# Prompt's merge products behind the sample's tiles, one block from merge to experts, and an output stage with the gate product first

## What is computed

```python
def encoder_layer(x, c, w_ada, b_ada, ...):
    mod = jax.nn.silu(c) @ w_ada + b_ada
    sh1, sc1, ga1, sh2, sc2, ga2 = jnp.split(mod[:, None, :], 6, axis=-1)
    h = rms_norm(x, g_pre1) * (1.0 + sc1) + sh1
    u = h @ w_in
    ...
    y_ret = retention_mixer(qr, kr, vr, gr, gn_ret)
    y_hg = hgrn2_mixer(qh, ih, ffh, fbh, gh, lb, gn_hg)
    merged = jax.nn.sigmoid(za) * (y_ret @ w_br_ret) + jax.nn.sigmoid(zb) * (y_hg @ w_br_hg)
    x = x + ga1 * rms_norm(merged @ w_out, g_post1)
    h2 = rms_norm(x, g_pre2) * (1.0 + sc2) + sh2
    x = x + ga2 * rms_norm(expert_choice_ffn(h2, w_router, w_gate, w_up, w_down), g_post2)
    return x
```

## Time and profile before

| what | us |
|---|---|
| median of 3 runs | 2843.82 |
| lowest and highest run | 2843.31, 2843.89 |
| the profiled execution | 2843.36 |
| its span, first to last instruction | 2841.4 |
| PE busy | 2655.7 (93%) |
| DVE busy | 1770.3 (62%) |
| ACT busy | 1338.3 (47%) |
| POOL busy | 301.7 (11%) |
| mean granted TensorE clock | 0.971 |

### The profile page before, as it was taken

The page is one execution under the profiler, slowest core; times in us unless marked ns, Lnnn a source line. Parts: engine busy times, 40 slices in busy tenths (PEclk is TensorE's granted clock), DMA queues, the critical chain, the costliest instruction groups (busy, mean ns, idle before and its releaser), DMA issues. The chain is left out here.

```text
span 2841.4 us, 48334 instructions
## 1 busy us (share of the span) xinstructions
PE 2655.7 (93%) x20554; PEld 2139.2 (75%) x20554; DVE 1770.3 (62%) x2140; ACT 1338.3 (47%) x1424; POOL 301.7 (11%) x246
## 2 busy tenths in 40 slices
PE   5999999999999998984999999999999999999993
PEld 2798888888888787873777777777777777777772
DVE  4575766757500053547777777777777777767775
ACT  5444535445211111453555555555555565555552
POOL 2010010101000021220011101110111101110110
PEclk8999999999999999996999999999999999999996
DMA  9211011111142165462888878888888888888886
GB/s 354 74 31 52 24 34 49 31 52 30 49 153 94 68 205 187 135 230 65 295 292 299 284 279 290 291 291 291 297 291 299 283 286 286 290 298 286 285 289 231
DMA packets 285510, 564.79 MB, mean 199 GB/s; under 512 B 24480, under 2 KB 90864, under 8 KB 285040
## 3 DMA queue, kind: packets, MB, share of 16 engines
q1 hardware_dynamic: 273216, 540.60, 53.9%
q0 software_dynamic: 7680, 20.98, 3.2%
q10 hardware_dynamic: 4400, 0.13, 0.1%
HBM read 514.44 MB, written 47.20 MB: 198 GB/s over the span
## 5 line engine op out<-in xcount | busy, mean ns | idle before, releaser
L2315 DVE TENSOR_TENSOR we_low<-ring,we_high 128x2048 fp32r<-128x2048 f32 x384 | 877.9, 2291 | 368.5 <-ACT we_high L2264 368.5
L2264 ACT ACTIVATE we_high<-ring 128x2048 fp32r<-128x2048 f32 x384 | 734.2, 1913 | 443.8 <-PE ps_ey L2236 279.8
L1335 PE MATMUL ps_a<-h_high,w_high 128*128 128x512 f32 (+1 forms) x696 | 252.7, 363 | 5.3 <-ACT pair L855 5.3
L1337 PE MATMUL ps_a<-h_high,w_low 128*128 128x512 f32 (+1 forms) x696 | 247.2, 355 | 0.0
L1336 PE MATMUL ps_a<-h_low,w_high 128*128 128x512 f32 (+1 forms) x696 | 247.2, 355 | 0.0
L2203 PE MATMUL ps_ep<-ring,xp 128*32 128x256 f32 x4096 | 234.3, 380 | 0.0
L2234 PE MATMUL ps_ey<-we_high,hidT_high 128*128 128x512 f32 x512 | 206.6, 403 | 0.0
L2178 PE MATMUL ps_eg<-we_high,xs_high 128*128 128x512 f32 x512 | 206.0, 402 | 0.3 <-DVE xs_low L2339 0.3
L2203 PEld LDWEIGHTS ps_ep<-ring,xp 128*32 128x32 f32 x4096 | 126.5, 110 | 99.5 <-issue 22.5
L2180 PE MATMUL ps_eu<-we_high,xs_high 128*128 128x512 f32 x512 | 200.2, 391 | 0.0
L2183 PE MATMUL ps_eu<-we_high,xs_low 128*128 128x512 f32 x512 | 200.2, 391 | 0.0
(11 more groups left out here) (324 smaller groups left out, 4975.1 us busy)
## 6 DMA issues: line engine op xcount, KB each, us to landing
ring<-in_w_gate SPq DMA_DIRECT2D x256, 512.0 KB, 10.2
ring<-in_w_up SPq DMA_DIRECT2D x256, 512.0 KB, 11.3
ring<-in_w_down SPq DMA_DIRECT2D x256, 512.0 KB, 5.8
w_raw<-in_w_in SPq DMA_DIRECT2D x52, 512.0 KB, 4.1
w_ring<-in_w_ada SPq DMA_DIRECT2D x20, 1024.0 KB, 8.8
sig_dram<-sig SPq DMA_DIRECT2D x15, 640.0 KB, 5.5
sig_g<-sig_dram SPq DMA_DIRECT2D x16, 512.0 KB, 4.0
yT_dram<-pair SPq DMA_DIRECT2D x8, 640.0 KB, 5.5
```

The source lines that it names most:

```text
L1335: pe.matmul(out, w_high, x_high, start=start, stop=False)
L1337: return pe.matmul(out, w_low, x_high, start=False, stop=stop)
L2264: act.activation(w_high[:, s % SPLIT], t.ring[:, s % RAW], ACT.Copy).then_inc(s_high, 1)
L2315: dve.tensor_tensor(w_low[:, s % SPLIT], t.ring[:, s % RAW], w_high[:, s % SPLIT], ALU.subtract).then_inc(s_low, 1)
```

## The change

`phase_merge`, `phase_route` and `phase_experts` become one block, `phase_tail`, with its SBUF laid out by hand (`place`) and the same eight PSUM banks throughout. The engines no longer meet between merge, tiles and experts. In it:

- **Merge**: 16 units, the sample's only. The splits of `w_out` stand beside it, one per output block (`out_weights_high`, `out_weights_low`). The sample's y stays in SBUF; the prompt's is loaded again later.
- **Tiles**: the sample's eight as before, except that there is one tile for the chunks of `w_ada`: chunk 0 is loaded by SP, chunks 1 to 3 by ACT, behind `modulate` of the same step.
- **Prompt's merge** (`prompt_merge`): behind the sample's last tile, eight times 24 products of 256 columns with weights loaded and split anew (`wp_raw`, `wp_high`, `wp_low`): high parts on ACT, low parts 0 and 1 on DVE, 2 to 7 on GpSimd. `turn` and `route` of tiles 6 and 7 stand between them. Then the prompt's two tiles, the first in two halves of the contraction; GpSimd makes the second half of their `m_low`.
- **To the first expert**: the prompt's tile 9 is scaled behind the sample's selection. The expert pieces 0 to 3 are split meanwhile: high on ACT, low of 0 and 1 on DVE, of 2 and 3 on GpSimd. The first gather takes the sample's rows alone. The prompt's selection (four rounds on DVE) stands behind `xs_low`, with its turns between the first expert's products; its rows (`x_rows(0, 2)`) are made on DVE behind the low part of piece 5.
- **Experts**: as before, but the prompt's scatter-add goes ahead of the sample's. `gate2` is loaded here.
- **Output**: ten loads of 0.5 MB. The product `moe * gate` comes first and no longer waits for the root: tiles 1, 4 and 7 on GpSimd, the rest on DVE; then one fused operation `gated * rstd + x1`.

The diff, cut to its core (functions that only moved are left out):

```diff
-            high(0)
-            for c in range(KC):
-                act.activation(t.w_out_high[:, c], t.w_out_raw[:, c], ACT.Copy).then_inc(s["wohigh"], 1)
...
-            def load_ada(i):
-                if i >= 2:
-                    sp.wait_ge(s["m"], i - 1)
-                sp.dma_start(w_a[i % 2][:], w_ada[i]).then_inc(s_wa[i % 2], 16)
...
+def phase_tail(nc, t):
...
+                if tl == 4:
+                    sp.wait_ge(s["mhigh"], NS_T)
+                    sp.wait_ge(s["mlow"], NS_T)
+                    for m in range(2):
+                        sp.dma_start(yp_raw[:, m], t.yT_dram[m].rearrange("h p n -> p h n")[:, :, NSAMPLE:NTOK]).then_inc(s["yp"], 16)
+                    for n in range(2):
+                        load_prompt_weights(n)
+                    for n in range(2):
+                        load_prompt_sig(n)
+                    sp.wait_ge(s["m"], PER)
+                    for n in range(2, NWP):
+                        load_prompt_weights(n)
...
+            prompt_weights_low(2)
+            prompt_weights_low(3)
+            residual(NS_T - 1)
+            prompt_merge(0)
+            prompt_weights_low(4)
+            prompt_merge(1)
+            prompt_merge(2)
+            prompt_weights_low(5)
+            prompt_merge(3)
+            prompt_weights_low(6)
+            prompt_merge(4)
+            prompt_weights_low(7)
+            for n in range(5, KC):
+                prompt_merge(n)
+            pool.wait_ge(s["ph"], 2)
+            pool.tensor_tensor(m_low[:, :, 4:KC], mergedP[:, 4:KC].rearrange("p c (x n) -> p x c n", x=2), m_high[:, :, 4:KC],
+                               ALU.subtract)
...
+            residual(NS_T)
+            gated(NS_T + 1)
...
+            gather(rows_s, t.idx_s, 0, s_rows_first, t.xn_dram[0:NSAMPLE])
+            pool.wait_ge(s_x[(NT - 1) % 3], 16 * ((NT - 1) // 3 + 1))
+            pool.tensor_tensor(x1[:, (NT - 1) % 3], x1[:, (NT - 1) % 3], x[:, (NT - 1) % 3], ALU.add).then_inc(s["x1"], 1)
...
+            piece_low(2)
...
+            pool.wait_ge(s["t"], 2 * NT)
+            piece_low(3)
+            pool.wait_ge(s["idxp"], 1)
...
+            def prompt_merge(n):
+                if n in (0, 1):
+                    pe.wait_ge(s["wplowd"], n + 1)
+                else:
+                    pe.wait_ge(s["wplowp"], n - 1)
+                if n == 0:
+                    pe.wait_ge(s["yplow"], 1)
+                    pe.wait_ge(s["scaled"], NS_T - 1)
+                if n >= 2:
+                    pe.wait_ge(s["pp"], n - 1)
+                for z in range(2):
+                    for c in range(HEADS):
+                        mm = split_products(pe, bank[n % 2][:, z * NPROMPT:(z + 1) * NPROMPT], wp_high[n % NWP][:, z, c],
+                                            wp_low[n % NWP][:, z, c], yp_high[:, 1 - z, c], yp_low[:, 1 - z, c],
...
+            pe.wait_ge(s_wolow, KC)
...
+            prompt_merge(0)
+            turn(NS_T - 2)
+            route(NS_T - 3)
+            prompt_merge(1)
+            prompt_merge(2)
+            route(NS_T - 2)
+            turn(NS_T - 1)
+            prompt_merge(3)
+            route(NS_T - 1)
+            prompt_merge(4)
+            prompt_merge(5)
...
+            mm.then_inc(s["at"], 1)
+            prompt_merge(6)
+            prompt_merge(7)
+            pe.wait_ge(s["scaled"], NS_T)
+            for h in range(2):
+                pe.wait_ge(s["ph"], h + 1)
+                pe.wait_ge(s["pl"], h + 1)
+                for hf in range(2):
+                    mm = out_part(NS_T, hf, 4 * h, 4 * h + 4)
+            mm.then_inc(s["o"], 1)
+            pe.wait_ge(s["pp"], KC)
+            out_part(NS_T + 1, 0)
+            out_part(NS_T + 1, 1).then_inc(s["o"], 1)
...
+            turn_x(0, 0)
+            route(NS_T + 1)
+            turn_x(0, 1)
...
+            gate_up(0, 0)
+            gate_up(0, 1)
+            pe.wait_ge(s["fp"], 1)
...
+            gate_up(0, 2)
...
+            gate_up(0, 3)
+            turn_x(0, 2)
+            gate_up_prompt(0)
...
+            for n in range(2, KC):
+                out_weights_high(n - 2)
+                branch_high(n)
+            out_weights_high(KC - 2)
+            out_weights_high(KC - 1)
...
+                if 2 <= k < 1 + PER:
+                    act.wait_ge(s["m"], k - 1)
+                    act.dma_start(w_a[:], w_ada[k - 1]).then_inc(s_wa, 16)
...
+            for n in range(1, KC):
+                parts(2 * n)
+                if n + 1 < KC:
+                    out_weights_low(n - 1)
+                    branch_low(n + 1)
+                if n == KC - 1:
+                    out_weights_low(KC - 2)
+                    out_weights_low(KC - 1)
+                    low(0)
+                parts(2 * n + 1)
...
+            piece_low(0)
+            piece_low(1)
+            variance(1, NS_T + 1)
+            modulate(NS_T + 1)
+            x_rows(0, 0)
+            dve.wait_ge(s["l"], NT)
+            centre(lg_p[:], ps_l[:, NS_T * NE:NT * NE].rearrange("p (k e) -> p k e", e=NE), mx_p, 2, s["smp"])
+            x_low(0, 0)
+            x_rows(0, 1)
+            prompt_share()
+            x_low(0, 1)
...
+                if b == 0:
+                    x_rows(0, 2)
...
-                dve.scalar_tensor_tensor(out=moe[:, tl], in0=moe[:, tl], scalar=ss[:, tl:tl + 1],
-                                         in1=gate[:, TILE_GROUP[tl]], op0=ALU.mult, op1=ALU.mult).then_inc(s_moe, 1)
-                if tl >= 1:
-                    residual(tl - 1)
...
+        POOL_TILES = (1, 4, 7)
+            for tl in POOL_TILES:
+                pool.wait_ge(t.s_ring[tl], loaded[tl])
+                pool.tensor_tensor(gated[:, tl], moe[:, tl], gate[:, TILE_GROUP[tl]], ALU.mult).then_inc(s_gated, 1)
...
+            def product(tl):
+                if tl not in POOL_TILES:
+                    dve.wait_ge(t.s_ring[tl], loaded[tl])
+                    dve.tensor_tensor(gated[:, tl], moe[:, tl], gate[:, TILE_GROUP[tl]], ALU.mult)
...
+            def total(tl):
+                if tl in POOL_TILES:
+                    dve.wait_ge(s_gated, POOL_TILES.index(tl) + 1)
+                dve.wait_ge(s_std, tl + 1)
+                dve.scalar_tensor_tensor(out=x1[:, tl], in0=gated[:, tl], scalar=ss[:, tl:tl + 1],
+                                         in1=x1[:, tl], op0=ALU.mult, op1=ALU.add).then_inc(s_y, 1)
+
+            product(0)
+            variance(0)
+            for tl in range(NT):
+                if tl + 1 < NT:
+                    product(tl + 1)
+                    variance(tl + 1)
+                dve.drain()
+                total(tl)
```

1246 lines of the change are left out of this document (655 added, 591 removed).

## The result

| | us |
|---|---|
| before, median of 4 runs | 2843.86 (2843.31 to 2846.33) |
| after, median of 4 runs | 2824.77 (2823.93 to 2825.83) |
| ratio | 0.9931, 95% interval 0.9914 to 0.9949 |
| the profiled execution after | 2824.14, span 2821.8 |

The change takes 19.1 us away (19.2 between the two profiled executions, for which 17.6 were forecast). Two terms of the forecast's sum were wrong, though, with opposite signs, and that is what most of the experiments are about.

A forecast was written before the change was run, and what follows sets the result against it. PE is full in the experts, so time moves only before the first expert's last product and after the last down; -37.8 + 11.0 + 0.9 + 9.4 - 0.8 - 0.3 = -17.6 gives 2826 us, range 2807 to 2837.

The forecast's parts named there:

- Merge to tiles, -37.8: Prompt products leave the merge and PE starts the tiles earlier at the high clock; tile 0 ends 37.8 us earlier.
- The chunks, +11.0: In the sample's tiles, w_ada chunks 1 and 3 land 5.1 and 3.3 us late, with one 2.6 us restart: +11.0 us.
- case A: Rival: chunks load in 4.8 us, GpSimd holds up nobody, PE's last wait keeps the clock: 2807 us; chance 0.28 with half ways.
- To the first expert, +0.9: From the last sample tile's end to the first expert's first product: 100.1 us against 99.2 before, +0.9 us.
- the shares are ready before it gets there; the selection starts at about 31: Behind the last sample tile: shares ready before PE ends 17.3 us of work, selection starting at about 31 us (before 34.4).
- case B: Rival: GpSimd bounds the prompt's products, and four of its operations meeting DVE's low halves cost 2.35 us each: 2835; chance 0.11.
- First expert, +9.4: First expert's start to the prompt's product: 26.4 us against 17.05, with a 4.9 us wait and the low clock; +9.4 us.
- Scatter, -0.8: After the experts: the prompt's scatter goes first, so the sample's has landed by 2802.1, before 2802.88; -0.8 us.
- Output, -0.3: Output stage: smaller loads gain 1.2 us, GpSimd's products of tiles 4 and 7 hold DVE, +0.9; together -0.3 us.
- terms 1, 4 and 5: Merge to tiles -37.8 us, first expert +9.4 us, and the scatter -0.8 us.
- signs of error: Wrong if tiles start after 8 us idle, no chunk is waited for, or the output stage is 4 us shorter.
- The price of a restart, 2.6 us: PE restarting at the low clock after idle time costs about 2.6 us, half of the 5.2 us it lasted.

The follow-up runs named there:

- e9: Changed kernel with ACT's issue of w_ada's chunk loads 1 to 3 two places earlier, ahead of norm of the step: 2824.88 us.
- e1: Changed kernel with GpSimd's low parts 2 and 3 of the prompt's branch weights moved behind tile 7's addition: 2817.32 us.
- e10: e8 plus e9's loads, tile 9 scaled with its gate on DVE, and the shares turned one prompt group earlier: 2807.88 us.
- e3: Changed kernel with x_rows(0, 2), the prompt's rows for the first expert, ahead of the split of piece 5 on DVE: 2820.09 us.
- e4: Changed kernel with all ten products of the output stage on DVE, none on GpSimd: 2823.57 us.
- e6: Changed kernel with ACT issuing w_ada's chunk loads 1 to 3 later, behind the squares of the next step: 2854.49 us.
- e8: Changed kernel with the edits of e1, e3 and e4, e2's splits on DVE, and the sample's rows ahead of the prompt's tile 9: 2807.33 us.
- e2: Changed kernel with the low parts of expert pieces 2 and 3 made by DVE, none by GpSimd: 2823.71 us.
- e5: Kernel before the change, with PE's wait for c_pad_c moved from the head of its list to the first chunk of w_ada: 2840.36 us.

## Why the prediction was right, and where it was not

The forecast said 2826 with 2807 to 2837; measured were 2824.8. Point by point:

1. **Merge to tiles, -37.8: right.** Tile 0 started 35.6 us earlier, behind a wait of 0.80 us (1.0 forecast). With the chunk's 1.2 taken out, tile 7 ended 37.7 us earlier.

2. **The chunks, +11.0: wrong, it was +1.2.** Two links failed. "ACT issues the next load behind `modulate`" is true of the list and not of the time: ACT's sequencer hands out a DMA while computations ahead of it wait their turn, so it left at 1128.79, 2.4 us before `modulate` ended (row in e9). And I took 7.5 us for the load, where the three took 5.9 (median). 5.0 us of lead less 6.1 of load is the 1.16 us of wait, too short for the clock. My case A came nearer on this point (3.0 us), with the shorter load but not the earlier issue. The Trainium skill, DMA: Bandwidth & Descriptors, section Bandwidth, gives 6.15 us for 1 MB, there issued from GpSimd. The measured 5.9 us, of loads issued by ACT, is near that, and not near the row of 8.1 us that I leaned on.

3. **To the first expert, +0.9: wrong, it was +10.9.** The step that failed is its first line, "the shares are ready before it gets there; the selection starts at about 31": it started 38.4 us behind tile 7's end. I had costed GpSimd's splits of the prompt's weights where they feed PE, and not where they stand beside DVE's, on the way of tile 7's variance; e1 shows 8.0 us for that, more than the whole error of this line (7.4): without these two splits in the way the choice starts 30.5 us behind tile 7's end, where I had 31. The lock itself was in the forecast (and case B), its place was not; and the larger part of its price, 10.9 us of PE at the low clock behind the wait of 4.76 us, was nowhere in it. Another 1.9 us: the choice lasted 43.8 us, not 42, with one operation ahead of `idx_s` held by GpSimd's `gated`:

```profile
1271.94 2.36 POOL L1750 TENSOR_TENSOR x_r<-x_r,gate 128x1024 f32<-128x1024 f32 x1 [9.52 <-ACT x_r L2158]
1272.35 1.98 DVE L2497 TENSOR_SCALAR place_s<-place_s 128x16 f32<-128x16 f32 x1 [0.43 <-issue]
```

It has one tile as input and is held all the same; without `gated` on GpSimd it takes 0.17 us (e10). The Trainium skill, SBUF — State Buffer, section Who interferes with whom, counts such an operation among those that can take the shared ports; this row agrees. From `idx_s` on the forecast held: 27.9 us measured, 27.1 forecast, with the operation of 0.69 us that I had named lasting 4.66. The wait for GpSimd's second half of `m_low` was 2.78 us (2.3 forecast), and the clock did fall behind it, for about 3.3 us, against what I had assumed:

```profile
1244.10 0.47 PE L1335 MATMUL bank<-w_out_high,m_high 128*128 128x512 f32 x1 [2.78 <-POOLq L1791]
...
1245.00 0.63 PE L1335 MATMUL bank<-w_out_high,m_high 128*128 128x512 f32 x1
```

That cost nothing, as PE then waited 7.34 us for DVE's choice.

4. **First expert, +9.4: right (+8.2).** The wait was 5.03 us for 4.9; 5.77 us of products for 6.2; e3 takes the low clock and 3.4 us of the wait away. The terms as I wrote them add up to 26.7, not 26.4.

5. **Scatter, -0.8: right (-0.9).** 6. **Output, -0.3: nearly (-0.9).** From the first use of a load to the end it was 0.9 us longer, as forecast, with two fused operations of 3.05 and 2.89 us; the load gave 1.8 and not 1.2. The parts were less good than their sum: I had put each lock at 2.35 us, which on top of 26.5 makes 31.2 and not the 30.6 I wrote; the two took 1.8 and 1.6. e4 gives the net price of using GpSimd there: 1.2 us.

So the total is as good as it is by luck: 9.8 us too much in one term met 10.0 too little in the next, and nothing ties the two together. What the forecast had right by its mechanism are terms 1, 4 and 5. Of what I had named as signs of error, one did occur in part: the chunks were hardly waited for.

The price of a restart, 2.6 us, was taken from one place. Other waits gave from about 2 (5.17 us of waiting in e6) to 6.5 (5.18 and 6.04 us there), so it is no constant, and a single row does not give it.

## What to carry to other kernels

Look at GpSimd's elementwise work beside every stretch where DVE's list is what others wait for, however small DVE's operations are: one of 0.16 us lost 2.2, and moving two splits by one place gave 7.5 us of the 17.4 that e8 adds to the change. Before removing a wait, ask what wait of the same length stands behind it on another engine (e2 removed 7.8 us of locks for nothing), price the low clock behind it by a range and not by one row, and where an engine starts late, read the releaser's line: it may wait for something that it does not need yet (e5).

## What was not expected of the hardware

- A DMA that ACT issues leaves while computations ahead of it in ACT's list have not run: 2.4 us before the end of `modulate` in the changed kernel, and 5.7 us earlier again when it stands ahead of `norm` and `modulate` (e9).
- How long TensorE stays at 1.2 GHz is not a matter of the idle time before alone: 3.3 us behind 2.78, 5.2 behind 3.89, 10.9 behind 4.76, 3.2 behind 5.07 in the changed kernel and 5.7 behind 5.07 in e9, 4 behind 5.17 and 13.0 behind 5.18 in e6, 5.3 behind 11.74; none behind 1.63 (e3) or 1.16.
- GpSimd's operation of 128x2048 fp32 took 4.52 us, and the two operations of DVE with two SBUF tiles that started in the time of such a one ended 0.5 to 0.6 us behind it, after 4.55 and 4.66 us where 0.69 is their length. DVE's one-input operation on 128x16 was held too: 1.98 us beside GpSimd's product, 0.17 without it (e10).
